# Modulation units taken slot by slot among the first tiles of two norms, one unit inside the last value slot, and two output splits moved ahead of later heads' maxima

## The chip, the cores and the metric

The kernel runs on one core of one Trainium2 chip. Times are device microseconds (us) of one execution. TensorE (PE) does matmuls, VectorE (DVE), ScalarE (ACT) and GpSimd (POOL) the elementwise work, and SyncE (SP) issues the weight loads. "PEld" is TensorE's load of the stationary operand. What counts is the device time of the whole program.

## What is computed

Two blocks on 256 tokens of width 1024. The first block has two layers over x and, in its first layer, over 256 context tokens too. Each layer is steered by a modulation of the conditioning vectors:

```python
def ada_modulation(cond, w, b):
    m = jax.nn.silu(cond) @ w + b          # w: 1024 x 6144, for c and for c_ctx
    return jnp.split(m, 6, axis=-1)        # shift, scale, gate of the mixer and of the FFN
def modulate(x, g, shift, scale):
    return rmsnorm(x, g) * (1 + scale[..., None, :]) + shift[..., None, :]
```

Layer 0 is gated linear attention ("gla") and a convolutional FFN; layer 1 is latent attention ("mla": down to ranks 384 and 256 plus 64 rotary columns, up to 8 heads, softmax over 512 keys, output projection) and an FFN on x alone. The second block ("sec") mixes banded attention of 8 heads, a convolution branch and attention to a memory of 256 tokens by 4 heads, then an FFN. Everything is held to float32 accuracy.

## The kernel before

**Weights** come as a stream of 384 slots of 128 x 1024 floats (512 KB) through a ring of RAWS = 8 raw buffers. SP issues the load of slot n (`load_slot`, L288) once the slot 8 places before it has been taken (`slot_used`, counted in the order TAKEN). `QUEUE` is the order of the slots, written by hand. An ordinary slot is split in two: ACT rounds it to `whi` (`hi_slot`, L296, ring of 4) and POOL forms the rest `wlo` (`lo_slot`, L301). TensorE then does three products for each tile, whi by the high and the low part of the activations and wlo by the high part, all in the fp32r form (L312).

**Modulation units.** A unit is 4 slots (512 columns of one `w_ada`). It is not split: `mod_products` multiplies the raw slot in plain float32 by a stationary operand of 32 columns. Row block k goes to column group k % 4 of the array, so that a slot (k = 2s and 2s + 1) uses two of the four groups. Each product shows in the trace as two records, a slot as 4 and a unit as 16 (L410). Unit 3 of layer 1 is used after the norm "ffn0", unit 7 after the norm "mix1", units 8 to 11 before and amid the first scores of mla. When four units are in, ACT copies the row (`mod_row`, L420) and TensorE turns it into columns (`mod_turn`, L426).

**Norms.** TensorE adds the squares over the partitions (L546), ACT forms the inverse root (L510, L514), DVE scales tile k (L592), ACT writes its high part (L562), DVE the low part (L579). `first_tiles` starts the next stage's first three weight tiles while these arrive: for each of 8 k it waits for `n_hi` and does six products (L357, L358), then three for the low part of k - 1 (L349). `keep_running` (L368) issues plain float32 matmuls of 256 columns (two records each) whose result nobody reads.

**mla.** After the first tiles three column tiles follow (m = 3 to 5), with sums of squares (L1160, `down_sums`) between them, whose inputs ACT evicts and squares (L1319, L1323). ACT does one `hi_slot` after each eviction in the same loop. DVE then normalizes (L1400 to L1411), and step s = 0 of the list `UP` (14 half slots: 6 of queries, 4 of keys, 4 of values) needs the third `cqlo`. After s = 12 the rotary swaps (L1233) are done; after s = 13 `keep_running(pe, 7, 4)`, units 8 and 9, then the scores (L1243, L1246), which need the rotated keys and the first normalized pair of heads (L1427); then units 10 and 11, then the transposes of the first softmax (`turns`, L1256).

**sec.** Heads go in pairs n = 0 to 5. ACT does exponentials (`exps`, L1748), evicts transposes (`turned`, L1756) and rounds outputs (`out_high`, L1761). DVE does maxima (`maxes`, L1905 and L1906), reciprocals (`recips`, L1912) and the low parts of outputs (`out_low`, L1916). POOL scales the probabilities of a pair after `recips` (`even_pair`, L1849), and TensorE's `turns` (L1697) waits for it. `outputs(n)` (L1712) waits for the low part of n - 1.

## Time and profile before

| | |
|---|---|
| median of 3 runs | 1368.34 us (1367.17 to 1374.93) |
| the profiled execution | 1368.0 us, its span 1366.2 us |
| mean granted TensorE clock | 0.996 |
| TensorE busy | 1331.7 us, 97% |
| VectorE, ScalarE, GpSimd busy | 579.1, 677.8, 706.7 us |
| TensorE's largest wait by cause | 20.7 us in 15 waits for raw slots of modulation units |
| HBM read | 208.15 MB, 153 GB/s over the span |
| chain that ended last | PE 92%, DMA 3%, ACT 2% |

The span runs from the first to the last instruction; the execution is 1.8 us longer. A start in the timeline is when the instruction began; matmuls overlap, so that the distance between two starts is what one costs, and not its duration. Idle time in brackets stands before the instruction, with what ended it.

### The profile page before, as it was taken

How to read it: one execution, taken by the hardware profiler on the slowest of the kernel's cores; microseconds unless marked ns; L12 is line 12 of the kernel's file. 1: busy time of each engine (PE TensorE's matmuls, PEld its weight loads, DVE VectorE, ACT ScalarE, POOL GpSimd, SP SyncE). 2: the span in 40 equal slices, each digit the busy share in tenths (PEclk: the TensorE clock that was granted, in tenths of full speed). 3: DMA queues.
4: the chain of work that ended last, by engine and by line, in shares of the span. 5: the costliest groups of instructions: out<-in, count | busy, mean ns of one | idle time of the engine just before them, and what ended most of it. 6: DMA issues, size and time to landing. Idle time of an engine off the chain costs nothing.

```text
span 1366.2 us, 22286 instructions
## 1 busy us (share of the span) xinstructions
PE 1331.7 (97%) x8270; PEld 1113.1 (81%) x8270; DVE 579.1 (42%) x1070; ACT 677.8 (50%) x1038; POOL 706.7 (52%) x307
## 2 busy tenths in 40 slices
PE   4999999999999999999999999999999999999999
PEld 0678787776888888888758746999999987999999
DVE  4414575324534443310035645455532485455510
ACT  1553134433544444432236845576675667666642
POOL 0433002243344444444344302598899775698897
PEclk9999999999999999999999999999999999999999
DMA  9423644253433333233454370566667541566564
GB/s 363 158 79 95 226 151 158 94 199 139 149 98 92 95 104 92 92 108 108 154 210 170 108 270 8 166 214 191 193 200 212 175 141 61 166 193 196 192 208 124
DMA packets 60118, 210.20 MB, mean 154 GB/s; under 512 B 6416, under 2 KB 9744, under 8 KB 59920
## 3 DMA queue, kind: packets, MB, share of 16 engines
q1 hardware_dynamic: 59616, 207.52, 46.0%
q10 hardware_dynamic: 432, 1.70, 0.3%
q8 instruction: 48, 0.79, 0.2%
q14 instruction: 22, 0.18, 0.0%
HBM read 208.15 MB, written 1.05 MB: 153 GB/s over the span
## 4 chain that ended last, share of the span: by engine, by line
PE 92%; DMA 3%; ACT 2%; SPq 1%; DVE 1%; issue 1%; POOL 0%; ACTq 0%
PE ps L312 72%; DMA raw<-wstream 3%; PE ps L410 2%; PE ps L933 2%; PE ps L357 1%; PE ps L927 1%; PE ps L358 1%; PE ps L919 1%; PE ps L349 1%; PE ps L1264 1%; SPq L288 1%; PE ps L1243 1%; PE ps L860 1%; PE ps L913 1%; PE ps L1224 1%
## 5 line engine op out<-in xcount | busy, mean ns | idle before, releaser
L301 POOL TENSOR_TENSOR wlo<-raw,whi 128x1024 fp32r<-128x1024 f32 x291 | 694.4, 2405 | 644.2 <-ACT whi L296 643.6
L296 ACT ACTIVATE whi<-raw 128x1024 fp32r<-128x1024 f32 x291 | 306.4, 1055 | 238.6 <-PE ps L312 143.9
L312 PE MATMUL ps<-Hhi_,whi 128*128 128x256 f32 (+1 forms) x1344 | 392.5, 320 | 0.0
L312 PE MATMUL ps<-Hlo_,whi 128*128 128x256 f32 (+1 forms) x1344 | 387.9, 316 | 0.0
L312 PEld LDWEIGHTS ps<-Hhi_,whi 128*128 128x128 f32 x1344 | 252.5, 188 | 26.7 <-issue 5.4
L312 PEld LDWEIGHTS ps<-Hlo_,whi 128*128 128x128 f32 x1344 | 252.5, 188 | 20.0 <-issue 1.9
L312 PE MATMUL ps<-Hhi_,wlo 128*128 128x256 f32 (+1 forms) x1344 | 233.6, 316 | 0.0
L312 PEld LDWEIGHTS ps<-Hhi_,wlo 128*128 128x128 f32 x1344 | 196.0, 188 | 18.4
L312 PE MATMUL ps<-hidhi,whi 128*128 128x256 f32 (+1 forms) x528 | 151.1, 315 | 0.0
L312 PE MATMUL ps<-hidlo,whi 128*128 128x256 f32 (+1 forms) x528 | 150.7, 314 | 0.0
L650 ACT ACTIVATE u<-ps,par 128x256 f32<-128x256 f32 (+1 forms) x132 | 83.8, 635 | 119.3 <-PE ps L312 110.4
L692 DVE SCALAR_TENSOR_TENSOR u<-ps,par,u 128x255 f32<-128x255 f32 (+1 forms) x132 | 75.4, 571 | 140.3 <-ACT u L650 139.7
L312 PEld LDWEIGHTS ps<-hidhi,whi 128*128 128x128 f32 x528 | 99.1, 188 | 8.5 <-DVE XT L784 1.7
L312 PEld LDWEIGHTS ps<-hidlo,whi 128*128 128x128 f32 x528 | 99.1, 188 | 6.9
L784 DVE SCALAR_TENSOR_TENSOR XT<-ps,ada,XT 128x256 f32<-128x256 f32 x48 | 21.7, 480 | 172.4 <-PE ps L312 168.4
L312 PE MATMUL ps<-hidhi,wlo 128*128 128x256 f32 (+1 forms) x528 | 91.5, 314 | 0.0
L410 PE MATMUL ps<-raw,cs 128*32 128x512 f32 x384 | 62.4, 647 | 21.4 <-DMA raw<-wstream 20.7
L695 DVE SCALAR_TENSOR_TENSOR u<-ps,par,u 128x255 f32<-128x255 f32 (+1 forms) x132 | 75.4, 571 | 18.6 <-DVE u L692 2.0
L312 PEld LDWEIGHTS ps<-hidhi,wlo 128*128 128x128 f32 x528 | 76.5, 188 | 6.9
L410 PEld LDWEIGHTS ps<-raw,cs 128*32 128x32 f32 x384 | 11.8, 113 | 59.5 <-DMA raw<-wstream 32.9
L704 DVE TENSOR_TENSOR hidlo<-ps,hidhi 128x256 f32 (+3 forms) x66 | 33.9, 513 | 48.3 <-ACT hidhi L659 48.3
L659 ACT ACTIVATE hidhi<-ps 128x256 f32 (+3 forms) x66 | 30.1, 457 | 45.2 <-DVE ps L700 45.2
(305 smaller groups left out, 1619.3 us busy)
## 6 DMA issues: line engine op xcount, KB each, us to landing
raw<-wstream SPq DMA_DIRECT2D x387, 512.0 KB, 3.6
XT<-x_t SPq DMA_DIRECT2D x1, 1024.0 KB, 10.7
XT<-ctx_t SPq DMA_DIRECT2D x1, 1024.0 KB, 12.1
memx<-mem_t ACTq DMA_DIRECT2D x1, 1024.0 KB, 5.5
out_t<-XT SPq DMA_DIRECT2D x1, 640.0 KB, 6.2
par<-params SPq DMA_DIRECT2D x1, 457.5 KB, 3.0
glac<-gla_consts SPq DMA_DIRECT2D x1, 384.0 KB, 9.7
out_t<-XT SPq DMA_DIRECT2D x3, 128.0 KB, 2.0
```

Source lines behind the costliest of these rows:

```text
L288: sp.dma_start(raw[:, n % RAWS, :], wstream[turns * RAWS + SRC[n]]).then_inc(raw_in[n % RAWS], 16)
L296: nc.scalar.activation(whi[:, n % RING, :], raw[:, r % RAWS, :], ACT.Copy).then_inc(S["hi_ready"], 1)
L301: nc.gpsimd.tensor_tensor(wlo[:, r, :], raw[:, r, :], whi[:, n % RING, :].bitcast(F32), ALU.subtract).then_inc(S["lo_ready"], 1)
L312: mm = nc.tensor.matmul(o, a, b, start=start, stop=stop)
L410: mm = nc.tensor.matmul(ps[32 * g:32 * g + 32, MOD_BANK[batch], :], cs[:, k, 6 - 2 * v:38 - 2 * v], raw[:, r % RAWS, 512 * (k % 2):512 * ( ...
L650: nc.scalar.activation(acc[:, j % 4, :], ps[:, j % 4, 0:ntok], ACT.Identity, scale=pdyn(f"cw{f}_1", i * 8 + j), bias=pdyn(f"cb{f}", i * 8 ...
L659: nc.scalar.activation(hi[:, i * 4 + q, :], ps[:, HID_BANK, 0:ntok], ACT.Copy).then_inc(S[f"{t}_hi"], 1)
L692: nc.vector.scalar_tensor_tensor(seg(acc, 1, T), seg(tile, 0, T - 1), pdyn(f"cw{f}_0", i * 8 + j), seg(acc, 1, T), ALU.mult, ALU.add).then ...
L695: nc.vector.scalar_tensor_tensor(seg(acc, 0, T - 1), seg(tile, 1, T), pdyn(f"cw{f}_2", i * 8 + j), seg(acc, 0, T - 1), ALU.mult, ALU.add). ...
L704: nc.vector.tensor_tensor(lo[:, k, :], hf, hi[:, k, :].bitcast(F32), ALU.subtract).then_inc(S[f"{t}_pair"], 1)
L784: ins = nc.vector.scalar_tensor_tensor(x, y, ada[L][:, bass.ds(m * 2 + 16 * part_ + h, 1)], x, ALU.mult, ALU.add)
L933: mm = nc.tensor.matmul(ps[:, OBANK[vt], ch * CH:(ch + 1) * CH], Sh[:, j, vt * P:(vt + 1) * P], qdec[:, b, ch * CH:(ch + 1) * CH], start=F ...
```

## The change

Five edits:

1. Unit 3 of layer 1 (norm ffn0) and unit 7 (norm mix1) are no longer done before `first_tiles`, but one slot each in its rounds k = 1 to 4. Before the first tiles there are now 8 and 7 idle matmuls in place of 3 and 2.
2. In the stream, unit 8 stands between the two value slots, and its products come before s = 13. The four idle matmuls after s = 13 go. Units 9 and 10 now come before the first scores (8 and 9 did), and unit 11 alone after them (10 and 11 did).
3. In mla's first loop ACT does the weight splits of m = 0, 1 and 2 together after the third eviction.
4. ACT's split of the last value slot moves from s = 5 to s = 7.
5. In sec, `out_high(0)` goes in front of `exps(3)` and `out_low(0)` in front of `maxes(4)`.

```diff
-QUEUE += ... whole("kpe", "uq", "uk", "uv")
-QUEUE += [unit(1, u) for u in range(8, 12)] + whole("mo", "up1", "dn1")
+QUEUE += ... whole("kpe", "uq", "uk")
+QUEUE += [("uv", "uv", 0, 1), unit(1, 8), ("uv_", "uv", 1, 1)] + [unit(1, u) for u in range(9, 12)] + whole("mo", "up1", "dn1")
-UNIT_AFTER = {"ffn0": 3, "mix1": 7}
-IDLE_AFTER = {"ffn0": (0, 3), "mix1": (7, 2), "ffn1": (0, 4), "sffn": (0, 4)}
+UNIT_AMONG = {"ffn0": 3, "mix1": 7}
+IDLE_AFTER = {"ffn0": (0, 8), "mix1": (7, 7), "ffn1": (0, 4), "sffn": (0, 4)}
@@ first_tiles, in the loop over k
                 if k >= 1:
                     low_part(k - 1)
+                if 1 <= k <= MOD_UNIT and norm in UNIT_AMONG:
+                    mod_products(pe, 1, UNIT_AMONG[norm], (k - 1,))
@@ mod_products
-        def mod_products(pe, layer, u):
+        def mod_products(pe, layer, u, slots=range(MOD_UNIT)):
-            for s in range(MOD_UNIT):
+            for s in slots:
@@ mla_pe
             for s, (n, half) in enumerate(UP):
                 bank = 2 * (s % 2)
+                if s == 13:
+                    pe.wait_ge(S["m_klog"], 4)
+                    mod_products(pe, 1, 8)
...
-            keep_running(pe, 7, 4)
-            mod_products(pe, 1, 8)
             mod_products(pe, 1, 9)
+            mod_products(pe, 1, 10)
             pe.wait_ge(S["m_rot"], 2)
             pe.wait_ge(S["m_ev"], 14)
             scores(0, 0)
             scores(0, 1)
-            mod_products(pe, 1, 10)
             mod_products(pe, 1, 11)
@@ mla_act
-                hi_slot(act, n + RING)
+                if m >= 2:
+                    for n1 in range(START["cq"] if m == 2 else n, n + 1):
+                        hi_slot(act, n1 + RING)
...
-                if half != 0 and n + RING < START["mo"]:
+                if half != 0 and n + RING < START["mo"] - 1:
                     hi_slot(act, n + RING)
+                elif n == START["uk"] and half == 1:
+                    hi_slot(act, START["mo"] - 1)
@@ sec_act
+            out_high(0)
             exps(3)
-            out_high(0)
@@ sec_dve
             maxes(3)
+            out_low(0)
             maxes(4)
             recips(3)
-            out_low(0)
@@ tensor_program
-                        if st in UNIT_AFTER:
-                            mod_products(pe, 1, UNIT_AFTER[st])
```

## Rows read from the trace of the kernel before

**Rows 1.** The page's first part: busy time, share of the span, instructions.

```profile
PE 1331.7 (97%) x8270; PEld 1113.1 (81%) x8270; DVE 579.1 (42%) x1070; ACT 677.8 (50%) x1038; POOL 706.7 (52%) x307
```

**Rows 2.** TensorE's timeline: start, length, instruction; a unit amid column tiles.

```profile
269.29 0.84 PE L312 MATMUL ps<-Hhi_,wlo 128*128 128x512 f32 x3
270.06 1.92 PE L410 MATMUL ps<-raw,cs 128*32 128x512 f32 x16
271.92 0.50 PE L312 MATMUL ps<-Hhi_,whi 128*128 128x512 f32 x1
272.26 0.40 PE L312 MATMUL ps<-Hlo_,whi 128*128 128x512 f32 x1
```

**Rows 3.** TensorE's timeline at the norm ffn0 and its first tiles.

```profile
332.10 1.46 PE L368 MATMUL ps<-con 128*128 128x256 f32 x6
...
339.14 0.50 PE L357 MATMUL ps<-Hhi_,whi 128*128 128x512 f32 x1
...
355.37 1.09 PEld L426 LDWEIGHTS ps<-sel,modrow 128*128 128x128 f32 x8
```

**Rows 4.** ScalarE's timeline at the norm ffn0: the first two tiles' high parts.

```profile
335.44 1.63 ACT L562 ACTIVATE Hhi_<-ps,ada 128x256 fp32r<-128x256 f32 x4 [0.95 <-DVE ps L592]
```

**Rows 5.** TensorE's timeline at the norm mix1, its first tiles and `down_sums`.

```profile
714.87 0.38 PE L357 MATMUL ps<-Hhi_,whi 128*128 128x256 f32 x1
...
723.60 0.95 PE L426 MATMUL ps<-sel,modrow 128*128 128x8 f32 x8
...
731.23 1.56 PE L1160 MATMUL ps<-Hf,con 128*128 128x256 f32 x6 [1.09 <-ACT Hf L1323]
```

**Rows 6.** ScalarE's timeline of the same stretch.

```profile
710.52 1.62 ACT L562 ACTIVATE Hhi_<-ps,ada 128x256 fp32r<-128x256 f32 x4 [0.95 <-DVE ps L592]
...
727.73 1.06 ACT L296 ACTIVATE whi<-raw 128x1024 fp32r<-128x1024 f32 x1 [3.33 <-DMA raw<-wstream]
```

**Rows 7.** Timeline of all engines, 735 to 745 us: the normalization of the queries' rank.

```profile
740.59 2.60 POOL L301 TENSOR_TENSOR wlo<-raw,whi 128x1024 fp32r<-128x1024 f32 x1 [2.29 <-ACT whi L296]
...
740.85 2.62 DVE L1405 SCALAR_TENSOR_TENSOR cq<-cq,par,mrq 128x256 f32<-128x256 f32 x1
...
743.83 0.43 DVE L1411 TENSOR_TENSOR cqlo<-cq,cqhi 128x256 fp32r<-128x256 f32 x1
```

**Rows 8.** TensorE's timeline from the last value half slot to the first transposes.

```profile
792.03 0.58 PE L312 MATMUL ps<-whi,ckvhi 128*128 128x512 f32 x1
...
794.98 1.89 PE L368 MATMUL ps<-con 128*128 128x256 f32 x8
796.80 3.64 PE L410 MATMUL ps<-raw,cs 128*32 128x512 f32 x32
800.37 1.98 PE L1243 MATMUL ps<-kn,mq 128*128 128x512 f32 x4
...
809.83 1.05 PE L410 MATMUL ps<-raw,cs 128*32 128x512 f32 x4 [0.23 <-DMA raw<-wstream]
811.11 1.05 PE L410 MATMUL ps<-raw,cs 128*32 128x512 f32 x4 [0.23 <-DMA raw<-wstream]
812.10 1.09 PE L1256 MATMUL ps<-con,Pm 128*128 128x128 f32 x8
```

**Rows 9.** SyncE's timeline, 796 to 800 us: issues of unit 10's loads and the next.

```profile
797.89 2.35 SPq L288 DMA_DIRECT2D raw<-wstream  x5
```

**Rows 10.** VectorE's timeline: two key normalizations, then the first rows of probabilities.

```profile
797.39 2.48 DVE L1427 SCALAR_TENSOR_TENSOR kn<-kn,par,Hf 128x1024 f32<-128x1024 f32 x2
...
807.76 0.88 DVE L1466 TENSOR_SCALAR Pm<-Pm,arec 128x512 f32<-128x512 f32 x2
```

**Rows 11.** Timeline of all engines in sec's attention, 1142 to 1150 us.

```profile
1145.96 2.04 POOL L1849 TENSOR_TENSOR Pb<-Pb,brec 128x512 f32<-128x512 f32 x2 [2.53 <-DVE brec L1912]
...
1146.33 1.08 PE L1712 MATMUL ps<-PTb,svt 128*64 128x256 f32 x8 [1.16 <-DVE Hlo_ L1916]
...
1148.41 1.09 PE L1697 MATMUL ps<-con,Pb 128*128 128x128 f32 x8
```

More of the change, by code:

```diff
@@ L72 @@
     QUEUE += [(f"dn0_{_j}" if _j else "dn0", "dn0", _j, 1)] + ([unit(1, DN0_UNITS[_j])] if _j in DN0_UNITS else [])
-QUEUE += [unit(1, 6)] + whole("cq") + [("ckv", "ckv", 0, 1), unit(1, 7), ("ckv_", "ckv", 1, 1)] + whole("kpe", "uq", "uk", "uv")
-QUEUE += [unit(1, u) for u in range(8, 12)] + whole("mo", "up1", "dn1")
+QUEUE += [unit(1, 6)] + whole("cq") + [("ckv", "ckv", 0, 1), unit(1, 7), ("ckv_", "ckv", 1, 1)] + whole("kpe", "uq", "uk")
+QUEUE += [("uv", "uv", 0, 1), unit(1, 8), ("uv_", "uv", 1, 1)] + [unit(1, u) for u in range(9, 12)] + whole("mo", "up1", "dn1")
 QUEUE += [("mk", "mk", 0, 2), ("mv", "mv", 0, 2), ("sglu", "sglu", 0, 4), ("sqm", "sqm", 0, 2),
```

## The prediction

> **What bounds the kernel now.** I read the page's busy shares first, then who waited for whom, then the timelines of the four places that the diff touches. TensorE is busy 97% of the span and every other engine about half of it [rows 1], so an edit pays only if TensorE starts something earlier there or does less. The idle time that can be won is small: 20.7 us in all for raw slots of modulation units (the table above), much of it at the kernel's start, which is not touched. At the norm ffn0 the first tiles start at 339.14 [rows 3], while the first high part was written by 335.44 + 0.82 = 336.26 [rows 4]: 2.8 us go to unit 3, whose slots arrive one by one. At mix1 it is 714.87 [rows 5] against 710.52 + 0.81 = 711.33 [rows 6]. Before the first transposes TensorE waits slot by slot for unit 11 until 812.10 [rows 8]. In sec it stands 1.16 us for the low part of the first heads' outputs [rows 11].
>
> **What a lone slot costs.** A unit of 16 records amid fp32r products takes 271.92 - 270.06 = 1.86 us from start to start [rows 2]; two units together 800.37 - 796.80 = 3.57 [rows 8]. A lone slot of 4 records takes 812.10 - 811.11 = 0.99 [rows 8]: more than half a unit for a quarter of the work. That fits the kernel: a slot fills two of four column groups, and its two records per product follow each other, so two neighbouring slots run side by side and a lone one does not. The changes of form cost too. Of the three records that begin at 269.29 the last starts at 269.29 + 0.84 - 0.39 = 269.74, and the second product behind the unit at 272.26: 2.52 us, less two ordinary steps of 0.227 (1.82/8, the step of the records of 794.98 as well), is 2.07 for an inserted unit [rows 2, 8]. The changes of form are thus 0.21 beyond the 1.86. A lone slot inserted in a full stream costs 0.99 + 0.21 = 1.20; I take 1.17, since the 0.99 may hold some of it, and four of them 4.7. The bounds: 0.46 a slot (1.86/4) if slots of later rounds still overlap something, 1.2 above.
>
> **Edit 1 at ffn0.** The first tiles took 355.37 - 339.14 = 16.23 us of unbroken products [rows 3]. They would start at 336.35 (the eight idle matmuls, 16 records of 0.227 from 332.10, end at 335.7 and don't delay them [rows 3, 8]). ScalarE writes a tile's high part every 1.6 us, TensorE needs 2.04 for a round, so nothing waits and all four slots lie on the path: 336.35 + 16.1 + 4.7 = 357.15 against 355.37, **+1.8 us**. With slots of 0.46 it would be 354.3, -1.0. What ends last before the first tiles is no longer the weights but the norm; what is saved there (2.8) is less than what the splitting adds.
>
> **Edits 1 and 3 at mix1.** With 256 columns the rounds are shorter: 723.60 - 714.87 = 8.73 us in all [rows 5]. Start 711.4, plus 8.6 and 4.7: 724.65, **+1.05**; with cheap slots the norm's own pace (about 1.57 us a tile, the low part of the last ready near 722.7) holds it at 723.1, -0.5. Behind it edit 3 counts. ScalarE stood 3.33 us for the weights of m = 4 before it could evict m = 1 and 2 [rows 6], and TensorE then 1.09 us at `down_sums` [rows 5]. With the three evictions first this wait goes: -1.09. Queued behind the moved splits are only the eviction of m = 3 and the next loads' splits, needed 7 us later. So TensorE is level again at m = 4. But the chain ScalarE (root), VectorE (normalization) starts from the slot that m = 3 frees, 1.05 later, and `cqlo` came only at 743.83 + 0.43 = 744.26 [rows 7] for a step that began near 744.9. TensorE would wait 0.2 to 0.4 there. I take **+0.2** for the whole place, with -0.9 and +1.1 as ends.
>
> In that chain VectorE's op at 740.85 took 2.62 us where its likes took 0.48, and it ends as GpSimd's split from 740.59 ends [rows 7]. Shifted by one microsecond an earlier op would meet the same split and the chain keeps its length, which is in the +0.2. The Trainium skill, "SBUF — State Buffer", section "SBUF: two separate sides", says that VectorE ops with two SBUF inputs and GpSimd ops hold a shared port for a whole instruction, whoever starts first, which the row bears out (2.62 us). By that rule the +0.2 stands; if instead the ops ran free of each other, the chain would end 2.1 us sooner and the place would come to 0.
>
> **Edit 2.** The value half slot s = 13 starts at 792.03 and takes 2.95 us to 794.98 [rows 8]. Unit 8 now begins there, say 792.2, so s = 13 starts at 794.05 and ends at 797.0; unit 9 follows, its weights long in, to 798.9. The 1.82 us of idle matmuls are gone. Unit 10 is the question, because the scores now wait for it. Its fourth slot takes the place that the last value slot frees at about 797.2, and the loads in front of it start when unit 8 frees its first. In the profile that is 797.89, 1.09 after the unit's start [rows 9]; the eight loads that begin then end with the slot of 811.11, spaced 811.11 - 809.83 = 1.28 [rows 8], so the fifth was usable at 811.11 - 3 x 1.28 = 807.3, 9.4 us after the first issue. Now the first issue is at 793.3, and the fifth load, unit 10's last slot, is usable near 802.7; between 802.0 and 802.7 if the first ones land quicker. TensorE starts the scores at 802.7 + 0.99 = 803.7, say **803.4, 3.0 us later** than the 800.37 of before, although all else would let it start by 800.9. The key normalization (797.39 + 1.25 = 798.6) is no bound [rows 10]. SP's queue holds only these loads, in order; POOL has none.
>
> Behind the scores: before, two units covered the maxima, exponentials and row scaling, and the weights were last (812.10). Now one unit of 1.9 us does, its four loads in by 793.3 + 14.5 = 807.8. The scaled rows were ready at 807.76 + 0.88 = 808.64 [rows 10]; everything in front of them on VectorE follows the scores, so they come at 811.6. The second head's transposes, at 812.56 before (812.10 and half of 0.93), can go at 811.7. So **-0.8**, and what ends last there is the softmax and no longer the weights. The ends: -3.5 if the scores start at 800.7 (rows ready at 808.95, second half at 809.05), and +4.0 if the loads keep their old times (unit 10 whole at 807.3 + 0.99 = 808.3, 7.9 later, rows at 816.5, second half at 816.6). ScalarE's split moved to s = 7 (edit 4) costs 1.05 us in an engine that stood idle before its next eviction and before its next logarithm; nothing waits.
>
> **Edit 5.** `outputs(1)` loses its wait, -1.16 [rows 11]. But `out_low(0)` now stands in front of two maxima and `recips(3)`, and waits itself for TensorE's outputs and ScalarE's rounding, about 0.5 us. `recips(3)` comes 1.1 us later, GpSimd's scaling at 1147.0 in place of 1145.96 ends at 1149.0, and the transposes of pair 3, at 1148.41, must have their second half wait for it until 1149.05: the stall moves one step down and is nearly as long (+0.15 there). ScalarE is then ahead for pairs 4 and 5, whose outputs waited 0.36. **-0.2**, between -1.1 and +1.0.
>
> **Sum:** +1.8 + 0.2 - 0.8 - 0.2 = +1.0 us. The profiled execution took 1368.0 (span 1366.2 and 1.8 around it), 0.3 under the median of 1368.34. Forecast **1369.0 us**, its own range 1367.5 to 1370.5.
>
> **The rivals.**
> - *Lone slots are cheap* (0.46 each). For it: two slots do run side by side. Against: 0.99 for one, at each place where one stands alone. ffn0 -1.0, mix1 -0.5, the rest as above: -2.5, **1365.5**. It ends on the other side.
> - *The weights of unit 10 land early*, scores at 800.7. For it: fewer loads are in flight in front. Against: 512 KB each 1.28 us, five of them. Then -3.5 in place of -0.8: **1366.3**. Decides: the fifth load usable before 800.
> - *The loads keep their old times*, so unit 10 in front of the scores is a plain loss: +4.0 in place of -0.8, **1373.8**. Against: the slots in front are free 4.6 us sooner. Decides: usable after 806.
> - *Both gains together*: -5.2, **1362.8**.
> - *Sec gets longer*: the rounding in front of exponentials pushes ScalarE's chain past TensorE's: +1.0 in place of -0.2, **1370.2**.
> - *The clock*: units in front of the first tiles kept TensorE at work, now idle matmuls do and some 1.4 us of idle follow at mix1. If the granted clock (mean 0.996) fell from 2.4 to 1.2 GHz over mix1's first tiles, their 8.7 us would double: **1377.7**. Against: the waits of 1.0 us between lone slots cost no clock.
>
> **How the numbers follow.** Chances: forecast 0.46, cheap slots 0.15, early weights 0.14, late weights 0.08, both gains 0.06, longer sec 0.07, clock 0.04. The range takes in the first two gains, the forecast, the longer sec and what lies half way to the late weights: **1363.6 to 1371.6**. The likeliest one's own is above. A measurement here tells 0.5%, 6.8 us, from no change, and only the clock case reaches that upward; downward it would need all gains at their ends (ffn0 -1.0, mix1 -0.9, scores -3.5, sec -1.1) and a little more. Faster 0.05, the same 0.89, slower 0.06.
>
> **What would show it.** First tiles at ffn0 starting 2.8 us sooner against the norm but lasting 20.8 in place of 16.2; each L410 group of four followed by the next product after about 1 us; no wait of L1160 for ScalarE; unit 10 taken slot by slot in front of the first scores, with a short idle for weights before each; transposes waiting for VectorE's scaled rows; the 1.16 us wait gone from `outputs(1)` and a similar one at the transposes of pair 3. I would be wrong if the first tiles last under 19 us, if the scores start within 9 us of unit 8's start, or if a clock under 1.00 stands in those slices.

## Result and profile after

| | before | after |
|---|---|---|
| median, first measurement | 1368.09 us (6 executions, 1367.14 to 1374.93) | 1377.30 us (6 executions, 1370.46 to 1378.92) |
| ratio after/before as recorded | | 1.0045, 95% interval 1.0025 to 1.0064 |
| the profiled execution, its span | 1368.0, 1366.2 us | 1370.9, 1369.1 us |
| mean granted TensorE clock | 0.996 | 0.995 |

The median stands 8.3 us above the forecast of 1369.0 and outside its range. The recorded ratios, here and below, are not the quotients of the medians (1377.30/1368.09 would be 1.0067); all of them lie within 1% of 1. The profiled execution of after is 1.9 us above the forecast and 2.9 us above that of before. The six times of after are 1370.46, 1370.86, 1377.07, 1377.53, 1377.74 and 1378.92: two groups, with nothing for 6 us between them. The profile caught the lower group. So there are two questions: where 2.9 us come from, which the traces show, and what puts four of six executions some 7 us higher. The legs below are of one trace each: the first leg alone, whose code is the same in all, runs from 330.9 to 333.1 us over the thirteen traces of this document, so that a total is less sure than the leg that an edit touches.

**Where the span went.** I cut both traces at the sums of squares of the five norms and took the differences of their starts. The rows of after, TensorE's timeline (start, length, instruction, idle before it):

```profile
331.25 1.13 PE L548 MATMUL ps<-rstd,con 128*128 128x512 f32 x2 [0.51 <-DVE rstd L543]
...
708.41 1.13 PE L548 MATMUL ps<-rstd,con 128*128 128x512 f32 x2 [0.51 <-DVE rstd L543]
...
880.93 0.70 PE L548 MATMUL ps<-rstd,con 128*128 128x256 f32 x2 [0.16 <-DVE rstd L543]
...
1066.53 0.70 PE L548 MATMUL ps<-rstd,con 128*128 128x256 f32 x2
```

The last ones, of sffn, begin at 1183.54. Before, the same sums began at 331.13, 706.02, 877.26, 1062.86 and 1180.67. Hence the legs, in us (the last one ends with the span):

| leg | before | after | difference |
|---|---|---|---|
| start to ffn0 | 331.13 | 331.25 | +0.12 |
| ffn0 to mix1 | 374.89 | 377.16 | +2.27 |
| mix1 to ffn1 (mla) | 171.24 | 172.52 | +1.28 |
| ffn1 to smix (FFN 1) | 185.60 | 185.60 | 0.00 |
| smix to sffn (sec) | 117.81 | 117.01 | -0.80 |
| sffn to the end (last FFN) | 185.53 | 185.56 | +0.03 |

**The norm ffn0**, TensorE's timeline of after:

```profile
332.21 3.62 PE L370 MATMUL ps<-con 128*128 128x256 f32 x16
336.73 0.47 PE L357 MATMUL ps<-Hhi_,whi 128*128 128x512 f32 x1 [0.90 <-ACT Hhi_ L564]
...
340.30 1.05 PE L412 MATMUL ps<-raw,cs 128*32 128x512 f32 x4
341.28 0.50 PE L357 MATMUL ps<-Hhi_,whi 128*128 128x512 f32 x1
...
357.99 0.84 PE L428 MATMUL ps<-sel,modrow 128*128 128x8 f32 x7
```

The first tiles begin at 336.73, and not at 339.14 [rows 3], now held by ScalarE and no longer by weights. Each lone slot takes 341.28 - 340.30 = 0.98, and the product behind it 0.34 where its likes take 0.23. They last 357.99 - 336.73 = 21.26 us; before, from 339.14 to the first product of L426 at 355.60, it was 16.46. So they start 2.53 sooner against the norm and last 4.80 longer.

**The norm mix1 and what follows**, TensorE, then ScalarE, GpSimd with VectorE, and TensorE again, after:

```profile
727.28 0.95 PE L428 MATMUL ps<-sel,modrow 128*128 128x8 f32 x8
...
733.66 1.02 PE L1162 MATMUL ps<-Hf,con 128*128 128x256 f32 x4
```

```profile
728.70 0.36 ACT L1322 ACTIVATE cq<-ps 128x256 f32<-128x256 f32 x1
...
731.22 1.06 ACT L296 ACTIVATE whi<-raw 128x1024 fp32r<-128x1024 f32 x1 [1.70 <-DMA raw<-wstream]
```

```profile
742.93 2.40 POOL L301 TENSOR_TENSOR wlo<-raw,whi 128x1024 fp32r<-128x1024 f32 x1 [1.12 <-ACT whi L296]
743.10 2.38 DVE L1417 CAST cqhi<-cq 128x256 fp32r<-128x256 f32 x1
...
747.55 0.29 DVE L1417 CAST cqhi<-cq 128x256 fp32r<-128x256 f32 x1
747.88 0.43 DVE L1418 TENSOR_TENSOR cqlo<-cq,cqhi 128x256 fp32r<-128x256 f32 x1
```

```profile
748.36 0.38 PE L312 MATMUL ps<-cqhi,whi 128*128 128x256 f32 x1 [0.60 <-DVE cqlo L1418]
...
780.35 1.12 PE L1229 MATMUL ps<-Hf,con 128*128 128x512 f32 x2 [0.37 <-DVE Hf L1429]
```

Measured from the norm's sums, the end of the first tiles comes at 727.28 - 708.41 = 18.87, before at 723.60 - 706.02 = 17.58 [rows 5]: +1.29. ScalarE evicts all three tiles before it waits for weights, and the 1.09 us wait of `down_sums` [rows 5] is gone. It comes back as 0.60 for `cqlo` and 0.37 one step further. The collision of VectorE with GpSimd's split has moved from the op of [rows 7] to a cast of one operand: 2.38 us where the next two casts take 0.29. Which op is caught changes from trace to trace, and with it the wait for `cqlo`. In the traces of experiments 3 and 7, whose code is the same here, the cast began a little before the split (743.90 and 743.20 against 744.00 and 743.49), the two-input op behind it was held (2.50 and 2.64 us), and the wait was 0.32 and 0.28:

```profile
743.53 2.64 DVE L1418 TENSOR_TENSOR cqlo<-cq,cqhi 128x256 fp32r<-128x256 f32 x1
```

The row is of experiment 7.

**The scores**, TensorE after:

```profile
793.89 1.88 PE L1238 MATMUL ps<-mq,mlac 128*128 128x512 f32 x4
...
796.13 1.92 PE L412 MATMUL ps<-raw,cs 128*32 128x512 f32 x16
797.99 0.51 PE L312 MATMUL ps<-whi,ckvhi 128*128 128x512 f32 x1
...
800.95 3.61 PE L412 MATMUL ps<-raw,cs 128*32 128x512 f32 x24
...
806.85 1.05 PE L412 MATMUL ps<-raw,cs 128*32 128x512 f32 x4 [1.01 <-DMA raw<-wstream]
807.83 1.98 PE L1248 MATMUL ps<-kn,mq 128*128 128x512 f32 x4
...
813.77 1.93 PE L412 MATMUL ps<-raw,cs 128*32 128x512 f32 x16
815.77 1.09 PE L1261 MATMUL ps<-con,Pm 128*128 128x128 f32 x8
```

The rotary swaps began at 790.08 before and at 793.89 now. Counted from there the scores are 13.94 us away, before 10.29 (800.37 [rows 8]): +3.65. The transposes are 21.88 away, before 22.02: -0.14. Unit 10's last slot is the one that holds the scores, 1.01 us in the row of 806.85.

**Sec**, TensorE after:

```profile
1148.68 1.08 PE L1719 MATMUL ps<-PTb,svt 128*64 128x256 f32 x8
...
1151.63 0.66 PE L1704 MATMUL ps<-con,Pb 128*128 128x128 f32 x4 [0.80 <-POOL Pb L1856]
1152.63 0.66 PE L1704 MATMUL ps<-con,Pb 128*128 128x128 f32 x4 [0.34 <-POOL Pb L1856]
```

`outputs(1)` starts without its wait of 1.16 [rows 11]; the transposes behind it now wait 0.80 + 0.34 = 1.14 for GpSimd. TensorE's waits for raw slots over the whole trace of after (us in total, times, longest) are 16.9 us where before had 20.7:

```profile
PE ps L412 <- DMA raw<-wstream: 16.9, 8, 7.7
```

The leg of sec is 0.80 shorter, and most of that is in none of the changed places. Twelve microseconds of its output projection, before and then after (busy us and records of PE, PEld, DVE, ACT and POOL, the granted clock, DMA share, GB/s):

```profile
1166.00:1178.00 12.00, 12.00 (x104) 12.00 (x103) 4.20 (x11) 7.64 (x12) 12.00 (x6) 1.00 0.77 263
1169.00:1181.00 12.00, 12.00 (x108) 12.00 (x108) 4.30 (x11) 8.06 (x14) 11.91 (x6) 1.00 0.79 267
```

TensorE is busy throughout at a granted clock of 1.00 in both, and yet does fewer products before: they follow each other at 117.8 ns there and at 113.3 in after. The last 200 products of the leg take 24.84 us in before and 24.21 or 24.22 in all twelve other traces, so 0.6 of the 0.8 is this step. What the step is comes up again in experiment 3.

### The profile page after: what moved, and what is told of

It is laid out like the page before. It is cut to its first block, busy times and chain, and to the rows that moved or that the text cites. A ratio compares the mean times of both kernels' runs of the same rounds, so it can differ in the third digit from the quotient of the medians.

```text
span 1369.1 us, 22308 instructions
## 1 busy us (share of the span) xinstructions
PE 1336.9 (98%) x8282; PEld 1115.4 (81%) x8282; DVE 578.5 (42%) x1070; ACT 678.1 (50%) x1038; POOL 706.3 (52%) x307
## 3 DMA queue, kind: packets, MB, share of 16 engines
HBM read 208.15 MB, written 1.05 MB: 153 GB/s over the span
## 4 chain that ended last, share of the span: by engine, by line
PE 92%; DMA 2%; DVE 2%; ACT 2%; SPq 1%; issue 1%; POOL 0%; ACTq 0%; DVEq 0%
PE ps L312 71%; PE ps L412 3%; DMA raw<-wstream 2%; PE ps L935 2%; PE ps L357 1%; PE ps L929 1%; PE ps L358 1%; PE ps L921 1%; PE ps L349 1%; PE ps L1269 1%; PE ps L1248 1%; SPq L288 1%; PE ps L862 1%; PE ps L1251 1%; PE ps L915 1%
## 5 line engine op out<-in xcount | busy, mean ns | idle before, releaser
L412 PE MATMUL ps<-raw,cs 128*32 128x512 f32 x384 | 62.5, 643 | 17.6 <-DMA raw<-wstream 16.9
```

The lines of the kernel that those rows point to most:

```text
L412: mm = nc.tensor.matmul(ps[32 * g:32 * g + 32, MOD_BANK[batch], :], cs[:, k, 6 - 2 * v:38 - 2 * v], raw[:, r % RAWS, 512 * (k % 2):512 * ( ...
```

## Experiments

All run on one chip per group, each group beside its own executions of before. A median over executions in two groups says little, as the first experiment shows, so I give the groups as well.

**1. The changed kernel once more, unchanged.** No edit.

> The changed kernel once more, nothing edited, because its six times fall in two groups (1370.5 to 1370.9 and 1377.1 to 1378.9) and one of the six of before (1374.9) also stands 7 us over the rest. Theory A, two levels in both kernels that the edits have nothing to do with: times of both kernels at a lower level (about 1367.5 and 1370.7) and about 7 us over it, in like shares. Theory B, the edits make the upper level more frequent (something in a changed stretch is lost by a hair and in most executions): the changed kernel mostly near 1377, the kernel before nearly always near 1368. If the profiled execution falls in the upper group, its trace against the one at hand shows where the 7 us lie: under B in or behind one of the changed stretches, under A anywhere.

Twelve executions: five from 1368.75 to 1370.72, seven from 1374.33 to 1378.56; the median, 1375.18, lies in the upper ones. Ratio 1.0019, interval 0.9998 to 1.0041. The 35 executions of before in this group do it too: 18 from 1366.78 to 1370.07 (median 1368.12), 17 from 1371.61 to 1379.76 (median 1374.11). So the kernel before has the upper group as well, in about half of its executions here, and the 1374.93 among the three times of before fits it. Lower group against lower group the change costs 1370.05 - 1368.12 = **1.9 us**, upper against upper 1376.41 - 1374.11 = 2.3. That the lower groups differ speaks for theory A; with seven of twelve in the upper one against 17 of 35, a small effect of the edits on the shares (theory B) isn't excluded.

Its profiled execution took 1374.33 with a third thing in it. TensorE's timeline at the scores, and the same stretch in windows (after the busy times the granted clock, then DMA share and GB/s):

```profile
808.58 1.33 PE L412 MATMUL ps<-raw,cs 128*32 128x512 f32 x4 [2.37 <-DMA raw<-wstream]
809.84 3.35 PE L1248 MATMUL ps<-kn,mq 128*128 128x512 f32 x4
```

```profile
800.00:806.00 6.00, 5.77 (x35) 1.86 (x33) 4.11 (x6) 1.02 (x1) 0.00 (x0) 1.00 1.01 406
806.00:812.00 6.00, 3.63 (x9) 1.27 (x8) 0.00 (x0) 0.00 (x0) 0.00 (x0) 0.77 1.01 409
```

TensorE stood 2.37 us for unit 10's last slot, 1.4 more than in the other trace, and the clock then fell to half: the four scores took 3.29 us from start to start in place of 1.91. The leg is 175.30 against 172.52: 1.4 of the 2.8 are the longer wait and 1.4 the clock. Both FFNs took 185.6 us in it, so this execution, the lowest of the seven, stands above the gap for a reason of its own.

**2. Edit 1 undone** (units 3 and 7 whole, in front of the first tiles).

```diff
-UNIT_AMONG = {"ffn0": 3, "mix1": 7}
-IDLE_AFTER = {"ffn0": (0, 8), "mix1": (7, 7), ...}
+UNIT_AFTER = {"ffn0": 3, "mix1": 7}
+IDLE_AFTER = {"ffn0": (0, 3), "mix1": (7, 2), ...}
```

> Edit 1 undone alone: units 3 and 7 stand whole in front of the first tiles again, with 3 and 2 idle matmuls. Theory 1, four lone slots cost more than the wait for weights that they replace: ffn0 gives back 2.4 us and mix1 1.3 and the 0.6 of waiting for the normalized rank, so the lower level is near 1366.5, against 1370.7. Theory 2, the 2.4 us at ffn0 come from idle matmuls or the norm and not from the lone slots: no more than 1 us comes back. For the upper level: if it is edit 1 that brings it, it goes with it (9 of 10 executions at the lower level).

Median 1370.81, ratio 1.0014 (0.9991 to 1.0037); seven executions from 1366.91 to 1370.90 (median 1368.97), five from 1373.98 to 1378.20. The leg from ffn0 to mix1 is 375.50 in place of 377.16, so 1.7 of the 2.3 us come back. The first tiles last 16.48 us again, as before (16.46), but begin 8.59 after the norm's sums where before had 8.01, because the unit's slots came later; experiment 4, with the same code there, has 8.49. So edit 1 costs 1.7 to 2.3 us here, by which trace one compares it with. The leg of mla is 172.51, unchanged, but with a fall of the clock in it that after's trace doesn't have:

```profile
711.67 4.37 PE L410 MATMUL ps<-raw,cs 128*32 128x512 f32 x12 [0.21 <-DMA raw<-wstream]
```

Three slots took 4.31 us from start to start (the next instruction begins at 715.98) in which the clock stood at 0.66 on average from 710 to 715; so what edit 1 costs in mla can't be read from this one trace. Five of twelve executions in the upper group: it doesn't go with edit 1. The lower one is at 1368.97, and not at 1366.5 as theory 1 had it.

**3. Unit 10 back behind the first scores**, all else as changed.

```diff
-            mod_products(pe, 1, 10)
             pe.wait_ge(S["m_rot"], 2)
             pe.wait_ge(S["m_ev"], 14)
             scores(0, 0)
             scores(0, 1)
+            mod_products(pe, 1, 10)
```

> Unit 10 behind the first scores again, the rest of the change as it is. Theory 1, the scores wait for unit 10's weights (they began 3.7 us later against the swaps) and that ate the gain of the earlier loads: scores start 5 us sooner, the transposes are then no longer held by the softmax, 3.5 us come back, lower level near 1367.2. Theory 2, the softmax chain on VectorE holds the transposes anyway: under 1 us, near 1370. If unit 10's wait brings the upper level, it goes here.

Median 1368.39, ratio 0.9990 (0.9971 to 1.0009); eight executions from 1367.43 to 1368.74, four from 1372.32 to 1375.44. TensorE's timeline at the same place:

```profile
794.68 1.88 PE L1238 MATMUL ps<-mq,mlac 128*128 128x512 f32 x4
...
803.59 1.98 PE L1248 MATMUL ps<-kn,mq 128*128 128x512 f32 x4
...
809.54 3.64 PE L412 MATMUL ps<-raw,cs 128*32 128x512 f32 x32
813.11 1.09 PE L1261 MATMUL ps<-con,Pm 128*128 128x128 f32 x8
```

The scores are 8.91 us behind the swaps (13.94 with unit 10 in front), the transposes 18.43 (21.88). The leg falls from 172.52 to 168.67, 3.85 us, as theory 1 said. Units 10 and 11 together, behind the scores, run without one wait, as their slots land while the scores run. Unit 8 amid the value slots, with its idle matmuls gone, thus brought 22.02 - 18.43 = 3.59 us (2.64 in the trace of 4), and unit 10 in front of the scores took 3.45 of them back. (With unit 10 in front, the traces of 5, 7 and 8 have 21.78, 21.55 and 21.33 from swaps to transposes, so the price is 2.9 to 3.5.) This kernel's mla is 2.57 us shorter than before's 171.24.

And its profile caught the upper group (1375.44). The legs show where it is: FFN 1 took 185.61, the last FFN **192.33**, where after had 185.56. Windows of equal length in the two FFNs, first of after, then of this kernel (PE busy and records, PEld, DVE, ACT, POOL, granted clock, DMA share, GB/s):

```profile
900.00:940.00 40.00, 40.00 (x355) 40.00 (x355) 20.08 (x45) 27.10 (x45) 35.96 (x16) 1.00 0.62 195
1220.00:1260.00 40.00, 40.00 (x355) 40.00 (x354) 20.49 (x44) 27.59 (x45) 35.26 (x16) 1.00 0.62 191
```

```profile
900.00:940.00 40.00, 40.00 (x355) 40.00 (x354) 20.31 (x44) 26.83 (x45) 35.95 (x16) 1.00 0.64 196
1220.00:1260.00 40.00, 40.00 (x342) 40.00 (x342) 19.73 (x43) 26.18 (x43) 33.98 (x15) 1.00 0.61 186
```

The reader is to see that TensorE is busy for all 40 us in each, at a granted clock of 1.00, and yet does 342 products in place of 355. No wait is in it. The step from one product to the next is longer, as in sec's output projection of before. Nine steps at the same place, after and this kernel:

```profile
1219.91 0.28 PE L312 MATMUL ps<-Hhi_,whi 128*128 128x256 f32 x1
...
1220.93 0.28 PE L312 MATMUL ps<-Hlo_,whi 128*128 128x256 f32 x1
```

```profile
1220.99 0.28 PE L312 MATMUL ps<-Hlo_,whi 128*128 128x256 f32 x1
...
1222.05 0.28 PE L312 MATMUL ps<-Hhi_,whi 128*128 128x256 f32 x1
```

1.02/9 = 113 ns against 1.06/9 = 118 ns. The leg's ratio, 192.33/185.56 = 1.036, is that of the counts, 355/342 = 1.038.

**4. The edits 1 and 5 undone and unit 10 back**, so that of the change unit 8 amid the value slots and the edits 3 and 4 are left.

> Edit 1 and edit 5 undone and unit 10 behind the scores: what is left is edit 3 (evictions first, -1.1), edit 4, and unit 8 in front of s = 13 without the four idle matmuls (-3.6 by my sum). Theory 1 says 1368.0 - 1.1 - 3.6 = 1363.3 at the lower level. The rival, that the stalls only move on to what follows (the normalization of the ranks, the softmax), says 1366 to 1368.

Median 1368.26, ratio 0.9973 (0.9954 to 0.9992). Legs: ffn0 375.39, mla 168.12, last FFN 192.36. The seven lowest executions run from 1365.25 to 1368.85, so the lowest is 1.5 us under the lowest of before in the same group, 1366.78, and without edits 1 and 5 and unit 10 in front the change is a gain. It is smaller than theory 1's (a lower level of 1363.3): mla is 3.1 us shorter than before's and not 4.7. From swaps to transposes it took 19.38 against the 18.43 of experiment 3, as units 10 and 11 took 4.51 us here and 3.57 there.

**5. Lone slots made pairs.** The slots of a unit go two and two, in the rounds k = 2 and k = 4.

```diff
-                if 1 <= k <= MOD_UNIT and norm in UNIT_AMONG:
-                    mod_products(pe, 1, UNIT_AMONG[norm], (k - 1,))
+                if k in (2, 4) and norm in UNIT_AMONG:
+                    mod_products(pe, 1, UNIT_AMONG[norm], (k - 2, k - 1))
```

> The changed kernel with the two units taken in two pairs of slots (0 and 1 in round k = 2, 2 and 3 in round k = 4) in place of four lone slots; nothing else. Theory 1, column groups: two neighbouring slots fill all four groups and take about as long as a lone one (0.98), so each norm has two insertions of about 1.2 us in place of four: the first tiles at ffn0 last 18.7 to 19.0 us in place of 21.3, those at mix1 end 1.3 to 2.4 us sooner against the norm. Lower level about 1370.1 - 2.3 - 1.5 = 1366.3. Theory 2, the cost is in the number of records or in waits between forms: the first tiles keep 21 us within 0.7, lower level about 1370.

TensorE at ffn0:

```profile
343.65 1.07 PE L412 MATMUL ps<-raw,cs 128*32 128x512 f32 x8
344.65 0.50 PE L357 MATMUL ps<-Hhi_,whi 128*128 128x512 f32 x1
...
356.90 0.95 PE L428 MATMUL ps<-sel,modrow 128*128 128x8 f32 x8
```

Two slots together take 1.00 us from start to start, as one alone does (0.98). The leg from ffn0 is 374.72 in place of 377.16 (-2.44) and 0.17 under before's; the leg of mla is 170.32 in place of 172.52 (-2.20). This rules theory 2 out: a lone slot pays for as much as two neighbouring ones. That the reason is the column groups is what the placing in the kernel says (two groups a slot, four a pair); a pair of slots in the same two groups, 0 and 2, was not run. The times: 1373.63 at the median, ratio 1.0014 (0.9984 to 1.0044), five executions from 1366.22 to 1368.00, seven from 1373.61 to 1380.65, while before in this group had 16 of 29 below 1370 (median 1367.81). Its lower group is 1.0 us under before's, and the median says the opposite.

**6. Pairs, and unit 10 back.** The edits of 3 and 5 together.

> Pairs of slots as in b1, and unit 10 behind the first scores. If the two terms add: b1 less 3.8, lower level near 1362.7, which would beat the kernel before (1367.9 at its lower level) and the changed one (1370.1). The rival, that the DVE chain of the normalized rank and not TensorE sets the time after mix1, says that the pairs save only at ffn0: near 1364.5.

Median 1366.95, ratio **0.9960 (0.9933 to 0.9988)**: 0.4% below before, with an interval clear of 1 and clear of that of after in experiment 1, on another chip. Six executions from 1363.32 to 1365.55 (median 1364.35, 3.5 under before's lower group of the same chip), six from 1368.36 to 1371.62. The lower level was expected near 1362.7, or near 1364.5 if the pairs saved only at ffn0; it is at the second, though mla's leg, 3.2 us under that of the pairs alone, has the saving of both. Legs: 374.70, 167.12, 185.61, 117.39, 192.37. The profile caught the long last FFN again.

**7. Edit 5 undone**, all else as changed; one execution.

```diff
-            out_high(0)
             exps(3)
+            out_high(0)
...
-            out_low(0)
             maxes(4)
             recips(3)
+            out_low(0)
```

> Edit 5 undone alone (both splits of the first heads' outputs behind the exponentials and maxima again). From the squares' sum of the norm smix to that of sffn the changed kernel took 117.0 us and the one before 117.8. Theory 1, edit 5 moves its stall one step down and is worth 0 to 0.3 us here: 117.0 to 117.3, and the 1.2 us wait of outputs(1) for the low part is back while the one of 1.1 us at the transposes of pair 3 for GpSimd is gone. Theory 2, edit 5 is what made the stretch 0.8 shorter: 117.8.

1370.88 us. The leg of sec is 117.12 against 117.01: 0.1 us. The wait of `outputs(1)` is back, 1.16 us, and the one of the transposes gone:

```profile
1149.85 1.08 PE L1719 MATMUL ps<-PTb,svt 128*64 128x256 f32 x8 [1.16 <-DVE Hlo_ L1923]
...
1151.93 1.09 PE L1704 MATMUL ps<-con,Pb 128*128 128x128 f32 x8
```

**8. A probe of the step in the last FFN.** One more float32 product of 128 columns, which nobody reads, in front of each of its last seven output tiles.

```diff
                 pe.wait_ge(S[f"{t}_dn"], m + 1)
+                if f == 2 and m >= 1:
+                    nc.tensor.matmul(ps[:, 0, 0:P], ones, con[:, 0:P], start=True, stop=True)
```

> A plain float32 matmul of 128 columns, whose result nobody reads, before each of the last seven output tiles of the last FFN; the rest is the changed kernel. Of the five traces of variants and two of the kernels themselves, all have one spacing of fp32r matmuls through the whole last FFN, 113.3 ns or 117.8 ns, 185.5 or 192.3 us in all: that is the 6.8 us between the two levels. Theory A, the spacing is a state of TensorE's pipeline that a matmul of another form draws anew: the spacing changes at some of the seven places, and the two levels of times smear into steps of 1 us. Theory B, it is fixed by something outside TensorE for the whole execution (memory, another engine's phase): one spacing throughout, two levels as before, both 1.5 us later for the seven matmuls.

Median 1373.11 of ten, 1371.09 to 1378.60, ratio 1.0018 (0.9993 to 1.0043). Its profile stood at 113 ns before and after each of the seven; the leg is 187.31, the 1.8 us of the inserted products. A form change inside the stage did not change the step in this trace. One trace says no more: it had the short step to begin with. The ten times are six from 1371.09 to 1373.17 and four from 1375.70 to 1378.60, which looks like two levels and not like theory A's smear.

**9. Pairs, unit 10 back, and edit 5 undone** (the diffs of 3, 5 and 7).

> The slots in pairs, unit 10 back behind the first scores, and now the two output splits of sec back in their old place too. Theory 1 (the splits are worth about 0.1 us): the leg of sec is 117.4 us as with the units before, the lower of the two levels of times stands at 1364.0 within 0.4 us, the upper some 7 us above. Theory 2 (the splits hide a gain in sec that only an undisturbed stream shows): the leg is 0.5 us or more longer and the lower level at 1364.6 or above.

Median 1369.91 (1363.62 to 1373.26), ratio 0.9984 (0.9966 to 1.0002). The leg of sec is 117.12 against 117.39 of kernel 6. The four lowest executions run from 1363.62 to 1365.37 (kernel 6: 1363.32 to 1364.50), the other eight from 1368.99 on. Edit 5 is worth nothing that shows in the leg: with it the leg of sec came out between 116.96 and 117.42 in nine traces (after's and eight experiments'), without it at 117.12, 117.17 and 117.12. Before's 117.81 stands outside both, so the 0.80 of the first table is not edit 5's: the step in the output projection has 0.62 of it. The stretch that edit 5 touches, from the 500th to the 650th of the leg's products, took 23.96 to 24.00 us in the nine traces with it and 24.08 or 24.09 in the four without (before's too): it is worth 0.1.

**10 and 11. What stands in front of the last FFN**, on kernel 6: 12 idle matmuls in place of 4 behind the last norm's sums, then none.

```diff
-IDLE_AFTER = {..., "sffn": (0, 4)}
+IDLE_AFTER = {..., "sffn": (0, 12)}
```

> As the pairs with unit 10 back, but with 12 idle matmuls in place of 4 behind the sums of the last norm, in front of the last FFN's first tiles. Theory 1 (the step of the last FFN's matmuls, 113 or 118 ns, is drawn when the stage begins and does not hang on what stands in front): times at two levels some 7 us apart, about half of the executions at each, both 0 to 1.8 us above those of the pairs. Theory 2 (the idle time of TensorE in front of the first tiles decides it, and more idle matmuls remove it): one level holds nearly all executions, 10 or more of 12.

> As the pairs with unit 10 back, with no idle matmuls at all behind the sums of the last norm, so that TensorE stands still there for as long as the norm takes. Theory 1 (the step is drawn when the stage begins, whatever stands in front): two levels some 7 us apart, about half of the executions at each, the lower at 1364 within 0.5 us. Theory 2 (the idle time in front decides): nearly all executions at one level, 10 or more of 12, and the opposite one of the kernel with 12 idle matmuls.

With 12: 1368.05 at the median, six executions from 1365.69 to 1367.31, five from 1368.79 to 1371.33 and one at 1374.34. With none: 1369.89, spread evenly from 1365.24 to 1375.94. Neither holds one level in ten of twelve, so the idle time in front doesn't decide. But the first of the two showed something new. FFN 1, 185.6 us in the other traces, took **190.68** here, and the last one 188.26, of which 2.7 are the longer idle matmuls:

```profile
900.00:940.00 40.00, 40.00 (x342) 40.00 (x341) 19.87 (x43) 26.47 (x43) 33.61 (x15) 1.00 0.60 185
1220.00:1260.00 40.00, 40.00 (x355) 40.00 (x354) 20.48 (x44) 27.58 (x45) 35.27 (x16) 1.00 0.63 189
```

So the long step belongs to no one stage. It stood in FFN 1 until 1016.3 us and gave way to the short one where two products of another kind stand between two output tiles, the sums for the next norm (its row in the timeline, then the window of 40 us behind it):

```profile
1016.33 0.60 PE L639 MATMUL ps<-rstd,con 128*128 128x256 f32 x2
...
1020.00:1060.00 40.00, 40.00 (x356) 40.00 (x355) 10.46 (x26) 21.19 (x32) 38.61 (x17) 1.00 0.70 210
```

In the other twelve traces the same two products leave the step at 113.3. Over all thirteen, the step is one value through every unbroken run of FFN 1 (1140 products up to those two, 395 behind them), of the last FFN (1536, or each piece between the seven of 8), and of the output projections of mla (144) and sec (120); mla's is at 117.8 in every trace, sec's in before's alone. In sec's first stage it changes from one projection to the next with no other product and no wait between: from 113 to 118 at 1078.0 in after, from 118 to 113 at 1074.7 in before. With no idle matmuls the profile showed a fall of the clock at 1182.1 us for 3.4 us, after 1.97 us of idle; it made that leg 186.83.

## Why the prediction failed

**The step that failed** is in "How the numbers follow": *a measurement here tells 0.5%, 6.8 us, from no change, and only the clock case reaches that upward*. The time was taken to be one value with a little noise, 1374.93 among the three times of before to be a stray, and the range was made of the edits' costs alone. The runs show in its place that an execution of this kernel, changed or not, mostly falls in one of two groups 6 to 7 us apart: 17 of 35 and 13 of 29 executions of before were in the upper one, 11 of 18 of after (one of these by the wait and the clock of experiment 1, and not by the step). (Beside experiments 9 to 11, 29 executions of before ran from 1367.04 to 1375.98 with no gap between; there the groups are blurred. And five executions, four of before and one of experiment 5, took 1379.5 to 1382.0, 11.6 to 14.2 us above the lower group: about twice the distance, as if both FFNs had the long step; no profile caught one.) Where both groups hold about half, the median falls in either. By the lower one after is at 1370.1, 1.1 us above the forecast and within its range, though the terms below show that this nearness is in part luck; in the first measurement four of six were in the upper. The 9.2 us between the two first medians are 2.8 from the lower group of before to that of after (1367.84 and 1370.66), and 6.4 from the group.

What the groups are, the profiles show for the executions that they caught. Four traces (experiments 3, 4, 6, 9) have the last FFN at a step of 118 ns and 192.3 us, all others at 113 ns and 185.5 (besides what 8, 10 and 11 added to it). The difference, 6.8 us, is about the distance of the groups, whose medians lie 6.0 to 6.4 apart, and the four are all in the upper part of their kernel's times. All four are of variants; no profile caught before or after itself in the upper group by the step. That the executions without a profile divide for the same reason is the likeliest reading and not shown one by one.

**The terms.**
- *ffn0, +1.8*: right in mechanism, measured +2.27, and confirmed from the other side by the pairs (-2.44 for the same work). The lone slot was sized at 1.17 us of path. It is 4.80/4 = 1.20, the upper end that I had given (+0.1 in all). The first tiles begin 336.73 - 331.25 = 5.48 after the sums, and I had 5.22 (+0.26). The rest, 0.13, is that the sum carried the products of the first tiles as 16.1 where its own row gave 16.23. (355.37 [rows 3] was the load of the next step's operand, 0.23 before its first product; that stood on both sides and fell out.)
- *mix1, +0.2 for the place*: the first tiles were +1.05 and are +1.29. The 1.09 us wait went, as said. What was mis-sized is what comes back: 0.60 at `cqlo` (0.2 to 0.4 worked out) and 0.37 at L1229, not foreseen. The 0.60 is no fixed price: it was 0.28 and 0.32 in two traces of the same code, by which op of VectorE met the split. To the rotary swaps it is 85.48 - 84.06 = +1.42 us: of the expected gain nothing was left. GpSimd's split did meet VectorE again, one op later, as expected.
- *Attention, -0.8*: measured -0.14 from swaps to transposes (-0.47 and -0.69 in the traces of 7 and 8). Scores +3.65 in place of +3.0: the last slot of unit 10 landed 0.2 us later than worked out from the first issue, unit 8 began 0.1 later, and I had rounded 0.3 away. From scores to transposes the working holds to 0.01 us (7.94 against 11.73 before, -3.79; the forecast had -3.8). The softmax rows don't hold them alone, though: unit 11 began at 813.77, a unit takes 1.86, and the first scaled row was ready near 815.7 too. The transposes begin 2.00 us behind unit 11's start, so the rows can hold them for 0.1 at most, and the wait for VectorE that was to be a sign of the forecast isn't in the trace.
- *Edit 5, -0.2*: worth 0.1 (experiment 9). The stall moved one step down, with its length (1.14 for 1.16).

The forecast's sum was +1.0. The legs give +2.9, of which 0.1 is the kernel's start and -0.8 the leg of sec. Of that leg 0.6 is luck: the execution of before that the forecast was built on had the long step in sec's output projection, and after's had not. What belongs to the two changed places is 2.27 + 1.28 = 3.55, against +1.2 forecast. That the edits' own cost was sized at about a third is the second failing, hidden in the total by the 0.8 of sec. Not all of the 3.55 is sure: the traces of 7 and 8 have mla at 171.67 and 172.06 with the same code, 0.8 and 0.5 less than after's.

**The rivals.** Cheap lone slots, early weights, both gains and a longer sec didn't come about. The clock at half over mix1's first tiles didn't either: it is 1.00 there in after. Falls of the clock do exist, behind the kernel's start in three traces, but for 3.4 us each and with a price of 1.3 to 1.4 us where it can be read (1 and 11), and they are not what divides the groups. **What stays open**: why the step is 113 or 118 ns at the same granted clock, and what draws it. The idle time before the stage doesn't decide it (10, 11). Other products within the stage left it alone seven times in 8 and changed it once in 10, so they are not enough by themselves.

## What to carry to other kernels

Look at the times of the kernel before one by one before a range is given: if they fall in groups, the prediction is a chance for each group with the change's cost on top, and small changes are compared group by group or leg by leg in traces. Work that is moved into a gap should go in pieces that fill the array by themselves: here two slots cost what one costs, and that alone turned +2.3 us into -0.2 at ffn0. And a unit whose weights land last belongs behind the work that others wait for: unit 8 into the gap gained 2.6 to 3.6 us, unit 10 in front of the scores took 2.9 to 3.5 of them away.

## Of the hardware

- At a granted clock of 1.00 and with no idle time, products of 256 columns follow each other at 113 or 118 ns, as a rule for a whole stage at a time: 355 or 342 records in 40 us, 185.5 or 192.3 us for an FFN. One trace switches inside a stage, at two products of another kind (1016.3 us of 10). The output projection of mla ran at 118 in all thirteen traces.
- Plain float32 products with 32 stationary columns: 0.98 us for one lone slot (two column groups), 1.00 for two side by side (four groups), 1.86 for a unit of four.
- TensorE's clock fell to half for 3.4 us after waits of 2.37, 1.99 and 1.97 us in three traces (the scores of 1, the unit in front of mix1's first tiles of 2, the last norm of 11), and stayed at 1.00 through waits of 1.01 and 1.34 us in after and of 1.49 us in that of 2 (at 336.07).
- A VectorE cast of one operand from SBUF took 2.38 us beside GpSimd's split of a weight slot, and 0.29 us without it; a two-input op took 2.50 and 2.64 us beside it, and 0.43 without. The Trainium skill, "SBUF — State Buffer", section "SBUF: two separate sides", counts VectorE ops in a two-port mode among those that hold the shared port, beside those with two SBUF inputs of which the prediction spoke; by that the row agrees. No row names the mode, but the times fit it: for 256 and 512 elements a free cast takes 0.29 and 0.43 us, a free two-input op 0.43 and 0.69, so the cast goes about twice as fast by the element. This one-input op, at least, is no escape from the collision.
